# Reordering the block between input projection and output projection of a hybrid diffusion step on one Trainium2 core

## The reference

```
h   = rmsnorm(x) * (1 + sc1) + sh1
z   = h @ w_in                    # 1280 columns: 512 ssm, 256 pool, 2 x 256 conv
ssm:  per group, bu = B u; h = scan(lam, bu) in both directions; y = Re(C h) + D u
      y = gelu(y); y = y * sigmoid(y @ w_glu + b_glu)
pool: windows 2/4/8/16: (mean - token) @ pool_w, times pool_scale
conv: v = a * sigmoid(g); depthwise conv, width 31; layer norm over channels; silu
x   = x + g1 * (concat(ssm, pool, conv) @ w_out)
x   = x + g2 * ffn(rmsnorm(x)...); out = rmsnorm(x)
```

## Time and profile before

| | |
|---|---|
| three timed runs | 1479.51, 1479.66, 1480.89 us; median 1479.66 |
| profiled execution | 1479.28 us, of which 1477.5 us are the profile's span |
| PE busy | 1349.0 us (91%) |
| PE weight loads | 1190.1 us (81%) |
| DVE, ACT, POOL busy | 571.9 (39%), 365.8 (25%), 385.1 (26%) |
| granted TensorE clock, mean | 0.93 of full |
| the stretch 207.8 to 503.9 us | input projection's last 17 blocks to the last modulation tile |

### The profile page before, as it was taken

How to read it: one execution, slowest core, us unless ns; L and a number is a source line. 1 busy time by engine, 2 the same in 40 slices (tenths; PEclk the granted TensorE clock), 3 DMA queues, 4 the chain that set the end, 5 groups by cost and what they waited for, 6 DMA issues and landing times.

```text
span 1477.5 us, 17898 instructions
## 1 busy us (share of the span) xinstructions
PE 1349.0 (91%) x7174; PEld 1190.1 (81%) x7174; DVE 571.9 (39%) x816; ACT 365.8 (25%) x610; POOL 385.1 (26%) x256
## 2 busy tenths in 40 slices
PE   3657998969996899999999999999999999999995
PEld 2147987868862478799999999999999999999894
DVE  2975479983048433322121212122222212121267
ACT  1254351221032534531211111111111111111116
POOL 0800015640022210043322223231313131313115
PEclk9779999985567899999999999999999999999998
DMA  8742154195345123222110101010101010111043
GB/s 271 253 160 63 47 182 137 57 175 158 91 163 237 57 86 123 82 74 78 29 57 28 57 28 57 28 57 28 57 28 57 28 57 28 48 37 43 0 144 128
DMA packets 100520, 130.02 MB, mean 88 GB/s; under 512 B 6270, under 2 KB 78248, under 8 KB 97784
## 3 DMA queue, kind: packets, MB, share of 16 engines
q1 hardware_dynamic: 99408, 126.88, 27.4%
q0 software_dynamic: 640, 2.36, 0.4%
q10 hardware_dynamic: 424, 0.12, 0.0%
HBM read 105.75 MB, written 23.59 MB: 88 GB/s over the span
## 4 chain that ended last, share of the span: by engine, by line
PE 78%; DVE 7%; issue 4%; POOL 4%; ACT 3%; DMA 2%; SPq 1%; ACTq 0%; DVEq 0%; POOLq 0%
PE banks L732 22%; PE banks L733 22%; PE banks L734 22%; DVE banks L1814 3%; PE banks L979 3%; PE banks L981 2%; PE banks L977 2%; DMA ldt<-in_ssm_log_dt 1%; PE banks L819 1%; PE banks L1014 1%; DVE acc L1939 1%; PE banks L1019 1%; ACT sq L1436 1%; SPq L402 1%; POOL psum_w L637 1%
## 5 line engine op out<-in xcount | busy, mean ns | idle before, releaser
L732 PE MATMUL banks<-nt_hi,f13h 128*128 128x384 f32 x1056 | 360.0, 341 | 3.8 <-POOL f13l L690 3.8
L734 PE MATMUL banks<-nt_hi,f13l 128*128 128x384 f32 x1056 | 356.9, 338 | 0.0
L733 PE MATMUL banks<-nt_lo,f13h 128*128 128x384 f32 x1056 | 356.9, 338 | 0.0
L1884 DVE TENSOR_TENSOR fv<-sa,banks 128x384 f32<-128x384 f32 x66 | 36.6, 554 | 486.1 <-PE banks L734 475.1
L732 PEld LDWEIGHTS banks<-nt_hi,f13h 128*128 128x128 f32 x1056 | 199.0, 188 | 5.4 <-issue 5.0
L733 PEld LDWEIGHTS banks<-nt_lo,f13h 128*128 128x128 f32 x1056 | 199.1, 189 | 0.4
L734 PEld LDWEIGHTS banks<-nt_hi,f13l 128*128 128x128 f32 x1056 | 199.2, 189 | 0.0
L696 POOL TENSOR_TENSOR f_lo<-fv,f_hi 128x384 fp32r<-128x384 f32 x66 | 68.2, 1033 | 398.9 <-ACT f_hi L1475 398.9
L732 PE MATMUL banks<-f2h,f_hi 128*128 128x512 f32 x396 | 154.9, 391 | 2.5 <-DVE te L1934 2.4
L733 PE MATMUL banks<-f2l,f_hi 128*128 128x512 f32 x396 | 154.2, 389 | 0.0
L734 PE MATMUL banks<-f2h,f_lo 128*128 128x512 f32 x396 | 154.1, 389 | 0.0
(11 more groups left out here) (275 smaller groups left out, 1772.9 us busy)
## 6 DMA issues: line engine op xcount, KB each, us to landing
fst<-in_ffn_w SPq DMA_DIRECT2D x66, 512.0 KB, 3.7
ad<-in_ada_w SPq DMA_DIRECT2D x20, 1024.0 KB, 8.4
wst<-in_w_in SPq DMA_DIRECT2D x10, 512.0 KB, 5.5
u<-z_dram SPq DMA_DIRECT2D x64, 72.0 KB, 2.6
kbw<-wc_dram SPq DMA_DIRECT2D x8, 576.0 KB, 5.3
wc<-wc_dram SPq DMA_DIRECT2D x16, 288.0 KB, 10.7
x_dram<-xr SPq DMA_DIRECT2D x9, 512.0 KB, 2.9
xe<-x_dram SPq DMA_DIRECT2D x9, 512.0 KB, 4.6
```

Of the source, the lines that this page charges most:

```text
L732: nc.tensor.matmul(out, hi_w, hi_x, start=start, stop=False)
L733: nc.tensor.matmul(out, hi_w, lo_x, start=False, stop=False)
L734: return nc.tensor.matmul(out, lo_w, hi_x, start=False, stop=stop)
L1884: TT(fv[b % 2][:, :], sa[b % 2][:, :], B[2 + b % 2][:, 0:BW], ALU.mult).then_inc(sem("f_made"), 1)
```

## The change

The lag kernels move forward: each `kb_half` and `ade_half` follows one projection block, from block 13 to block 20, and the last nine blocks run without them. SP's `w_in_load` for the weights of i = 7, 8, 9 moves behind `kb_weights`. The six pooling tiles move from behind the read-out to in front of it, into banks 3 and 7; the read-out's banks are turned round (`YB`), and it waits for the pooling tiles' evacuation. `ymp` and the output weights get other places, so that six of the eight output weights load later. The convolution's halves get a tile each: `cacc0` lies where the pooling's input was and waits for the pooling tiles, `cacc1` stays in `u9`'s place and waits for the read-out. The state copies are dealt out anew: POOL does both directions of pieces 0 and 2, ACT those of 1 and 3.

```
-    cacc = at("cacc", [P, 2, VO], O_UZ + 9216)
+    cacc = [at("cacc0", [P, VO], O_WB + 4608), at("cacc1", [P, VO], O_UZ + 9216)]
-    ymp = at("ymp", [P, 2, T], O_NT + 18432)
+    ymp = at("ymp", [P, 2, T], O_WS)
-    YB = (3, 5, 6, 7)
+    YB = (5, 6, 3, 7)
...
         for i in range(8):
-            sp.wait_ge(*low_ready(i))
-            w_in_load(i + 2)
+            if i < 5:
+                sp.wait_ge(*low_ready(i))
+                w_in_load(i + 2)
...
                 kb_weights(n)
+                if n >= 1:
+                    sp.wait_ge(*low_ready(i))
+                    w_in_load(i + 2)
...
-            if j == 1:
-                out_weights(2)
-                out_weights(3)
+            if j == 0:
+                out_weights(0)
+                out_weights(1)
...
-        for e in range(4):
+        for e in (0, 2):
             for r in range(2):
-                q0 = NPAIR + 4 * e
...
+                for d in range(2):
+                    q0 = NPAIR * d + 4 * e
...
-        z_block(13)
-        pe.wait_ge(sem("z_evac"), 10)
-        ade_half(0)
-        z_block(14)
-        ade_half(1)
...
-        for n in range(4):
-            kb_half(n, 0)
-            z_block(15 + 3 * n)
...
-            z_block(17 + 3 * n)
...
-        for s in range(27, 30):
+        for m in range(8):
+            z_block(13 + m)
+            ade_half(m)
+            kb_half(m // 2, m % 2)
+        for s in range(21, 30):
             z_block(s)
...
+        pe.wait_ge(sem("scan_done"), 1)
+        for j in range(2):
+            pe.wait_ge(sem("pooled"), j + 1)
+...
         pe.wait_ge(sem("toep_in"), 256)
...
+        pe.wait_ge(sem("pool_evac"), 6)
         for c in range(8):
...
-                pe.wait_ge(sem("st_copied_act"), 2 * (j + 1))
-                pe.wait_ge(sem("st_copied_pool"), 2 * (j + 1))
+                pe.wait_ge(sem("st_copied_act" if j % 2 else "st_copied_pool"), 4 * (j // 2 + 1))
...
-                    if j == 0:
-                        dve.wait_ge(sem("y_done"), 8)
-                    STT(cacc[:, j, :], src, w, csum, ALU.mult, ALU.add).then_inc(sem("tap_done"), 1)
+                    dve.wait_ge(*((sem("pool_done"), 6) if j == 0 else (sem("y_done"), 8)))
+                    STT(cacc[j][:, :], src, w, csum, ALU.mult, ALU.add).then_inc(sem("tap_done"), 1)
```

More of the change, by code:

```diff
@@ L470, in _ @@
             ada_in(n)
[L471 to L472 removed]
+        out_weights(2)
+        out_weights(3)
         for r in range(2):
@@ L956, in gate_rows @@
             last.then_inc(sem("gate_rows"), 1)
+        pe.wait_ge(sem("scan_done"), 1)
+        pe.wait_ge(sem("kb_evac"), 8)
+        pe.wait_ge(sem("wpool_in"), 64)
+        for j in range(2):
+            pe.wait_ge(sem("pooled"), j + 1)
+            for b in range(NB):
+                n = NB * j + b
+                if n >= 2:
+                    pe.wait_ge(sem("pool_evac"), n - 1)
+                bank = B[(3, 7)[n % 2]]
+                if b < 2:
+                    last = mm(bank[:, 0:BW], wpool[:, j, :], pu[:, j, PZ + b * BW:PZ + (b + 1) * BW], start=True, stop=True)
+                else:
+                    mm(bank[:, 0:256], wpool[:, j, :], pu[:, j, PZ + 768:PZ + LAT], start=True, stop=True)
+                    last = mm(bank[:, 256:BW], wpool[:, j, :], pu[:, j, PZ + LAT + PZ:PZ + LAT + PZ + CTX], start=True, stop=True)
+                last.then_inc(sem("pool_done"), 1)
         pe.wait_ge(sem("toep_in"), 256)
-        pe.wait_ge(sem("scan_done"), 1)
         pe.wait_ge(sem("z_evac"), 30)
-        pe.wait_ge(sem("kb_evac"), 8)
+        pe.wait_ge(sem("pool_evac"), 6)
         for c in range(8):
@@ L984, in _ @@
         pe.wait_ge(sem("y_evac"), 16)
[L985 to L998, removed]
         for r in range(2):
@@ L1018, in channel_mean @@
             for j in range(2):
-                last = mm(B[b][:, 0:389], onesm[:, :], src[:, j, 389 * b:389 * b + 389], start=(j == 0), stop=(j == 1))
+                last = mm(B[b][:, 0:389], onesm[:, :], src[j][:, 389 * b:389 * b + 389], start=(j == 0), stop=(j == 1))
             last.then_inc(sem("channels_meant"), 1)
@@ L1302, in _ @@
         v_out(3)
-        for s in range(12, 15):
-            z_out(s)
[L1305 to L1315, removed]
+        z_out(12)
+        for m in range(8):
+            z_out(13 + m)
+            if m in (1, 4, 7):
+                w_high(6 + m // 3)
+            kb_evac(m // 2, m % 2)
+        for s in range(21, 30):
+            z_out(s)
+            if s == 23:
+                w_high(9)
         def wo_high(n):
-            act.wait_ge(sem(f"w_in{n % 2}_in"), 80 + 16 * (n // 2 + 1))
+            act.wait_ge(sem(WO_IN[n][0]), WO_IN[n][1])
             nc.scalar.copy(wo_hi[n][:, :], wos[n][:, :]).then_inc(sem("wo_hi"), 1)
@@ L1323, in state_copy @@
             for r in range(2):
-                A_(view(sst, (r * Q + 4 * e) * UC, [[UC, 4], [BL, NBL], [1, BL]]),
-                   view(st, r * Q * SLOTS + 4 * e, [[1, 4], [Q, NBL], [SLOT, BL]]), ACT.Copy).then_inc(sem("st_copied_act"), 1)
+                for d in range(2):
+                    q0 = NPAIR * d + 4 * e
+                    A_(view(sst, (r * Q + q0) * UC, [[UC, 4], [BL, NBL], [1, BL]]),
+                       view(st, r * Q * SLOTS + q0, [[1, 4], [Q, NBL], [SLOT, BL]]), ACT.Copy).then_inc(sem("st_copied_act"), 1)
         def y_out(c):
@@ L1339, in _ @@
         act.wait_ge(sem("scan_done"), 1)
-        state_copy(0)
+        for j in range(2):
+            for b in range(NB):
+                n = NB * j + b
+                act.wait_ge(sem("pool_done"), n + 1)
+                A_(ymp[:, j, b * BW:(b + 1) * BW], B[(3, 7)[n % 2]][:, 0:BW], ACT.Copy, scale=pv[:, V_PS + j:V_PS + j + 1]).then_inc(sem("pool_evac"), 1)
         state_copy(1)
@@ L1351, in _ @@
         y_out(7)
[L1352 to L1356, removed]
         act.wait_ge(sem("fin_turned"), 1)
@@ L1379, in conv_silu @@
             act.wait_ge(sem("ln_scaled"), j + 1)
-            for dst, done in ((y_hi[6 + j], "conv_hi"), (cacc[:, j, :], "conv_out")):
+            for dst, done in ((y_hi[6 + j], "conv_hi"), (cacc[j][:, :], "conv_out")):
                 for c0, o, m in ((0, 0, LAT), (VCTX, LAT, CTX)):
```

43 lines of the change are left out of this document (18 added, 25 removed).

## The result

The changed kernel takes 1472.95 us (median of 9 runs, 1467.0 to 1475.31) where the kernel before, run beside it, takes 1480.47 (9 runs, 1477.93 to 1482.37). The ratio is 0.9945, 95% interval 0.9931 to 0.9959. So it is faster, as forecast, but by 7.5 us and not by 21.3: 1472.95 lies above the range of 1450 to 1468. The profiled execution took 1474.6 us, its span 1472.8.

What follows compares the result with a forecast made beforehand. The prediction took PE, busy 91% of the span, as the bound, through its idle stretches and low clock. Gains of 4.0, 3.3 and 14.0 us took 1479.28 to 1458.0, 1458.4 as median; range 1450 to 1468.

Steps and rivals of the forecast that it cites:

- Part 1: Blocks and lag kernels up to the last block: 103.5 to 106.7 us against 109.6, taken as a gain of 4.0.
- the forecast's 8.0 us: New cost in the blocks with lag kernels: 2.3 + 0.3 + 3 x 1.8 us, mainly waits for `kbw`.
- the slower rival: At the lag kernels, `kbw` loads of 7.6 us bring waits and low clock; slower from 5.3 us a round; chance 0.04.
- the forecast's signs of being wrong: Read-out of 50 to 60 us at 1.00, L900 waits over 3 us with falling clock, `ad` wait, last block after 317.
- Part 2: From the last block to the read-out: 8.0 us where it was 11.3, a gain of 3.3.
- Z + 8.0: Z is the last block's end; POOL's four copies end, and the read-out begins, 8.0 us after it.
- The rival in which `wc` comes late by itself: Before the read-out, the wait stays and the 3.3 us gain is lost: 1461.7 us; chance 0.12.
- Part 3: The read-out: same 160 matmuls at clock 0.50 again, 95.9 us, after 3.5 us of PE idle time.
- 0.08 for the rival: Read-out keeps the full clock through the 3.5 us idle: 48 to 58 us for 95.9, total 1416; chance 0.08.
- Part 4: Behind the read-out: DVE wait gone, -14.0 - 2.6 + 2.6 = -14.0 us, bounds -10 and -17.
- The sum: Whole kernel: -4.0 - 3.3 - 14.0 = -21.3 us on the profiled 1479.28, giving 1458.0.

Runs made afterwards that it cites:

- experiment 2: Only the new order of blocks, modulation halves and lag kernels, put into the kernel before: 1487.81 us, ratio 1.0051.
- experiment 1: Changed kernel with the old order of blocks, modulation halves and lag kernels on PE, ACT and SP: 1466.05 us, ratio 0.9907 to the kernel before.
- experiment 4: Changed kernel with each `kbw` half loaded once its place is free, ahead of `kb_out`, the first ahead of `ade`; kernel halves one block later: 1449.15 us.
- Experiment 7: Changed kernel, but the last tap of the convolution's first half waits for the whole read-out again: 1485.96 us, ratio 1.0022 to the kernel before.
- experiment 6: Changed kernel with the read-out's 64-row matmuls alternating between upper and lower half of the rows: 1417.65 us, ratio 0.9575 to the kernel before.
- e8: Changed kernel with the lag kernels' operand loaded early and the read-out's matmuls interleaved by row halves: 1398.98 us, ratio 0.945 to the kernel before.

## Why the prediction failed, step by step

**Part 1 is the step that failed.** It was forecast as a gain of 4.0 us and is a loss of 13.4 (123.0 against 109.6): the new waits for `kbw` were put too short, and the low clock behind them was put at nothing. The stretch came out 17.4 us over its forecast of 105.6, and that is made up of three terms: 6.5 for the waits (11.8 measured, 5.3 forecast), 12.3 for the clock (nothing forecast), less 1.4 for the work (98.9 measured, 100.3 left of the forecast without its waits).

*The waits.* The first was forecast as 2.3 us and was 3.87: the load came at 217.2, and I had taken 215.5. For the others I had 6.4 us from the evacuation of a finished kernel to the next one's first matmul, against 5.4 of PE's own work. The work was right (7.41 - 2.05 = 5.36 in the first of these rounds). The chain took 7.4, 8.6 and 8.1 us (230.95 to 238.36, 250.99 to 259.54, 272.11 to 280.16). I had let the landing of 5.3 us count from the first of the two issues; it counts from the second, 0.6 later, and it was 6.0 in the median and not 5.3. The forecast also has nothing but `kb_out` in the queue at these issues, and the trace has a load of `ade` (512 KB) 2 us ahead of them (230.06, 250.10, 271.22). Whether that slowed them is not shown. One term of the forecast's 8.0 us, 0.3, has no row behind it. What I knew, that each wait can only be late, I paid for with less than 1 us.

*The clock.* The 8.0 us of new cost in the forecast hold nothing for it. It was put into the slower rival, "the one buffer of `kbw`", with a chance of 0.04 and on condition that all loads take 7.6 us. The mechanism of that rival is what happened; its condition was wrong. Waits of 2.05 to 3.87 us were enough, and a fall cost 3.1 us where the rival had 3.3. Waits and clock are 24.1 / 4 = 6.0 us a round. Beyond the 1.3 us of wait a round that the sum held already that is 4.7, just under the 5.3 from which the change would have been slower. The row to see it by stood there: one wait of 6.1 us and 3.3 us of low clock behind it. I used it to explain the old stage and didn't price the new waits with it. Two of the forecast's signs of being wrong came with it: a wait of over 3 us with the clock falling, and a last block that ends later than 317. The Trainium skill ("TensorE: Matmul & The Clock Gate", "Why this matters for your kernels") advises against idle gaps between bursts. I weighed it for the read-out and not for this part; the runs bear it out here, with 12.3 us.

**Part 2 was right.** Z + 8.0 forecast, Z + 8.1 measured, with POOL's fourth copy as the last to end. The rival in which `wc` comes late by itself did not happen: from issue to landing it took 5.9 us in the median, where it took 10.7 before, and in experiment 2, where nothing else was late, PE waited 6.6 us for it (forecast 7.2). With the old order it is still late (experiment 1), for the old reason.

**Part 3 was right, and nearer the edge than its 0.08 for the rival says.** The read-out ran at 0.50 for 95.5 us. But filling 3.5 us turned it into the rival: 51.8 us where 54 was worked out (with 0.3 us a change of rows that stand in no row shown), and 1427.94 us; with experiment 4's edit 1409.77. The forecast of 1416 had assumed a part 1 that wins.

**Part 4 was right:** 14.5 us forecast as 14.0. DVE's wait is gone, the channel means took 4.09 us and not 6.69, and `glu_tile(0)` took 10.24 for 8.01, 2.2 us where 2.6 was charged. Experiment 7 takes the convolution's edit alone back and loses 13.0 by the medians, 11.7 by the means. The conditions came out otherwise than forecast: the first half's taps begin at 323.7 and not at 306, and its slack covered that (20.8 us of idle time in front of the last tap).

**The sum.** The error of the profiled execution is 1474.6 - 1458.0 = 16.6 us; the last block's end alone is 17.4 us later than forecast.

## What to carry to other kernels

Price an idle gap of PE at what it costs twice: its length, and the low clock behind it (here 11.8 and 12.3 us for four gaps of 2 to 4 us). If a wait is new in a forecast, take the clock's fall as the rule and its absence as the luck (16 of 20 here). Before work is moved closer together, move the loads that it needs: against the old order the new one gains 17 us with the operand early (1466.05 to 1449.15) and costs 7 with it late. How much of the 17 the old order would give as well, with its own late load (`ade`, 7.2 us of wait) moved forward, was not tried. Where matmuls use only half of the rows, alternate the halves (6.47 to 3.74 us for a chunk here).

## What the runs showed of the hardware

- The same sequence of matmuls, busy without a break, ran 95.5 us at 1.2 GHz after a gap of 3.5 us and 51.8 us at 2.4 GHz without the gap. Each level held to the end, in seven profiles with a gap in front and in two without.
- The interleaved sequence rose from 0.50 to 1.00 by itself, within 7 us of its start (experiment 6 and `e8`), and again behind its wait for `u`. That the order of half-array matmuls decides whether the clock rises is shown; why is not.
- 64-row matmuls on different halves of the rows overlap: 3.74 us for a chunk that took 6.47 at the same clock.
- Behind PE waits of 2.05 to 4.15 us the clock fell in 16 of 20 cases: in all four rounds of three profiles, in three of one and in one of another. Waits of the same length went both ways; what decides this stays open.
